# A two-block transformer kernel: 64 instead of 32 tokens of the expert layer go by gathered rows, and VectorE takes the low weight part first

## The chip, the core and the metric

The program runs on one core of a Trainium2 chip. The metric is the device time of one execution in microseconds: 3372.93 us before the change (median of 3 runs, 3371.32 to 3374.62). Engines are named as in the profile: PE is TensorE, PEld its weight loads, DVE is VectorE, ACT is ScalarE, POOL is GpSimd, SP is SyncE.

## What is computed

Two blocks over 256 tokens of width 2048 in f32. The change touches only the expert layer (PEER) of the first block. Each token has 8 heads, each head picks 16 of 16384 experts, and an expert is one row of `peer_u` and one of `peer_v`:

```python
expert = e1 * PEER_NKEYS + e2                 # 128 * 128 experts
gate = jax.nn.softmax(sv, axis=-1)            # over the 16 of a head
u = exp_u[ec]                                 # rows of 2048
a = jax.nn.gelu(jnp.einsum('cd,chkd->chk', xc, u))
w = gc * a
out = jnp.einsum('chk,chkd->cd', w, exp_v[ec])
```

After that come `x = x + g2 * out`, the final norm of the block and the whole second block (convolutions, gates, an MLP).

## The kernel before

**Two ways through the expert layer.** Most tokens go the dense way. The kernel multiplies them with all 16384 expert rows and masks the result with a routing matrix. The last `ROWS_T = 32` tokens go by rows. The kernel gathers the 128 rows that a token has picked, takes dot products with them, and adds the weighted rows of `peer_v`. `DENSE_T = 256 - ROWS_T = 224` is the number of columns of every dense matmul of the layer.

**The stream.** Weights come as units of 2 MB from HBM. A unit is split into two f16 halves. ACT writes the high part (`hi`, L1837, two instructions), and DVE the low part (`low`, L1077, two instructions). SP loads the next unit into a raw slot when the low part of the one before it there is done, and there are two raw and two split slots. PE then runs 96 matmuls of 128x128 weights per unit (L530, L531, L532). The layer has eight stages of 16 units: u0, u1, v0, u2, v1, u3, v2, v3. A u stage makes activations for one quarter of the experts, and a v stage sums one quarter into the output. One unit with what goes beside it is a *slot*. In slot n DVE makes the low part of unit n+2.

**Routing steps.** A stage that makes a quarter ready for its v stage (u1, v0, v1, v2) has `STEPS = DENSE_T // 16 = 14` routing steps, one per slot in slots 0 to 13. A step of 16 tokens is: DVE compares indices (`hot`: L1547 and L1549), POOL multiplies the first one-hot with the gates (`hot1_step`: L2209, twice), PE makes 32 small matmuls (`route`, L566), DVE multiplies with the activations (`gated`, L1556), ACT writes the high half (L2055), DVE the low half (`gated_low`, L1562). In a v stage DVE also adds the output to the residual (`residual_v`, L1568).

**Rows.** POOL's queue issues for each row token a gather (`row_load`, L2217, 128 rows of 8 KB, 1 MB) and, for the u rows, a load of the token's h vector copied to 128 partitions (`h_load`, L2222, 1 MB). DVE takes the dot product (`row_dot`, L1511) in u2, u3 and v3. PE multiplies with the v rows (`row_product`, L577) in v1, v2 and v3. POOL runs all of this and the 56 `hot1_step` calls in one written order. ACT does `row_gelu` and evicts the sum (`row_out`), PE turns it, and DVE adds it (`add_rows`, L1530 to L1539) near the end of v3. In u0 DVE also picks the experts (`select`, L1450 to L1486). The order on each engine is written out by hand, with semaphores between the engines.

The functions that the change touches:

Of the kernel before, what the change touches and what calls it, by code (L numbers as in the profile page):

```python
# [30 lines left out]
U32 = mybir.dt.uint32  # L31
# [23 lines left out]
ROWS_T = 32  # L55
# [129 lines left out]

def route_steps(n):

    return [n] if n < STEPS else []

ROW_GROUPS = [(0, 12), (12, 24), (24, 32)]
ROW_BATCHES = [(0, 12), (12, 24), (24, 28), (28, 32)]
ROW_LAST = {29: 0, 30: 1}

def row_loads():

    loads = []
    for n, (a, b) in enumerate(ROW_GROUPS):  # L200
        loads += [("u", i, i % 2) for i in range(a, b)]
        if n < 2:
            loads += [("v", i, i % 2) for i in range(a, b)]
        else:
            loads += [("v", i, ROW_LAST.get(i, 2)) for i in range(a, b)]
    place, count = {}, [0, 0, 0]
    for kind, i, buf in loads:
        count[buf] += 16
        place[kind, i] = (buf, count[buf])
    return place  # L210

ROW_PLACE = row_loads()

# [28 lines left out]
def program(nc, xT_d, wst, cst_d, dyn1_d, dyn2_d, dyn3_d, onehot_d, bmat_d, cmat_d, urow_d, vrow_d, skew_d, hrow_d, out_d):  # L244
    ctx = ExitStack()
    with ctx:
# [81 lines left out]
        row_buf = [A[:, 14336:16384], J[:, 0:2048], J[:, 4096:6144]]  # L328
        h_rep = J[:, 2048:4096]
        h_row = J[0:ROWS_T, 0:2048]  # L330
        ident16 = dyn[:, 320:384].bitcast(F16)
        dots = small[:, 0:ROWS_T]
        row_w = [h_rep[:, 0:384], h_rep[:, 0:384], J[:, 6144:6272], J[:, 6272:6400]]
        row_w = [w.rearrange("p (i t) -> p i t", t=ROWS_T) for w in row_w]
        row_out = J[:, 2048:2560]
        row_tmp = J[:, 2560:3072]
        x_rows = X[:, :].rearrange("p (k t) -> p k t", k=KT)[:, :, DENSE_T:T]
# [13 lines left out]
        row_index = gates.rearrange("p q h c -> p (q h c)").bitcast(U32)[:, 0:ROWS_T]  # L351
# [38 lines left out]
        def key_scores(h):  # L390
# [40 lines left out]
        row_in = [sem(f"row_in{i}") for i in range(3)]  # L431
# [4 lines left out]
            sem("rows_added"))  # L436
        merged, out_ready, relu_sb = sem("merged"), sem("out_ready"), sem("relu_sb")
# [49 lines left out]
        def _(pe_):  # L487
# [55 lines left out]
            def unit_u(s, bank):  # L543

                for m in range(2):
                    for k in range(KT):
                        hl = tuple(half[:, 0:DENSE_T] for half in halves(H, k))
                        mm = product(psW[:, bank, m * T:m * T + DENSE_T], s, k * 256 + m * P, hl, k == 0, k == KT - 1)
                return mm
# [417 lines left out]
            for u in range(32):  # L967
# [3 lines left out]
                if u == 0:  # L971
                    key_head(7)
                for qb in range(2):
                    if u == 9 + 8 * qb:
                        turn_picks(qb)
                if u >= 16:
                    for step_n in route_steps(u - 16):
                        route(step_n)
                if 20 <= u < 24:
                    h_rows(u - 20)  # L980
            for q in range(4):
                v0 = FIRST[f"v{q}"]
                pe_.wait_ge(acts_ready, STEPS * (q + 1))
                for n in range(16):
# [1438 lines left out]
```

## Time and profile before

| | us |
|---|---|
| median of 3 runs | 3372.93 |
| the profiled execution | 3384.46 |
| its span, first to last instruction | 3381.6 |
| PE busy | 3246.4 (96%) |
| DVE busy | 2354.0 (70%) |
| ACT busy | 1231.1 (36%) |
| POOL busy | 623.1 (18%) |

The expert layer starts with the first matmul of u0 at 718.92 us and ends with the first matmul of the next stage (z) at 2072.12 us. That is 1353.2 us of the span. PE's busy share is a poor guide here, since its instructions overlap and their ends are modelled. Starts of the same instruction one unit apart tell the pace. A row of the timeline gives start and duration in us, then engine, line, operation, output and input names with shapes, a count, and in brackets the idle time before it and what ended it. Because DVE instructions overlap a little at their ends, what one costs its successor is the distance of two starts.

A row of the windows view gives a stretch of the span and its length in us, the busy time of PE, PEld, DVE, ACT and POOL in it (with the number of instructions), the granted clock of PE as a share of 2.4 GHz, the busy share of the 16 DMA engines, and GB/s.

### The profile page before, as it was taken

The page shows a single profiled execution, that of the slowest core. Times are in us where ns is not written, and L with a number is a line of the kernel's source. Part 1 is how long each engine was busy: PE and PEld are TensorE (multiplying, and loading weights), DVE is VectorE, ACT ScalarE, POOL GpSimd, SP SyncE. Part 2 cuts the span into 40 slices and gives each one's busy share as a digit, 9 for nine tenths or more (in the row PEclk, how much of TensorE's full clock was granted, in tenths as well). Part 3 has the DMA queues.
Part 4 walks back from the last instruction along what each step waited for, and adds up shares of the span by engine and source line. Part 5 has one row for each costly group of instructions (what it writes and reads, how often), then busy time and mean ns, then how long its engine had stood idle before and what let it go on. Part 6 is the DMA issues. An engine that isn't in the chain of part 4 may idle for free.

```text
span 3381.6 us, 70432 instructions
## 1 busy us (share of the span) xinstructions
PE 3246.4 (96%) x31230; PEld 2906.9 (86%) x31230; DVE 2354.0 (70%) x2542; ACT 1231.1 (36%) x1126; POOL 623.1 (18%) x390
## 2 busy tenths in 40 slices
PE   7999999999999999999999988999999999999998
PEld 4777768789899999899989967888888788888887
DVE  7596145799998966895689667478758665554444
ACT  2010142444444444334433424344443433333332
POOL 0276000000354512471247110020000000000000
PEclk9899999999999999999999989999999999999999
DMA  9557694445455579777978884555545455555553
GB/s 410 236 222 293 278 419 153 175 175 217 183 201 202 203 290 423 278 278 297 426 261 289 349 321 175 199 199 199 198 175 202 172 199 198 201 199 205 202 203 132
DMA packets 66046, 814.77 MB, mean 241 GB/s; under 512 B 7354, under 2 KB 9418, under 8 KB 10512
## 3 DMA queue, kind: packets, MB, share of 16 engines
q1 hardware_dynamic: 48528, 700.47, 54.6%
q0 software_dynamic: 15008, 109.10, 8.3%
q8 instruction: 173, 2.83, 0.3%
q10 hardware_dynamic: 2304, 2.10, 0.2%
q14 instruction: 33, 0.27, 0.0%
HBM read 807.71 MB, written 3.93 MB: 240 GB/s over the span
## 4 chain that ended last, share of the span: by engine, by line
PE 73%; DVE 16%; DMA 7%; issue 2%; ACT 1%; ACTq 0%; DVEq 0%; POOL 0%; SPq 0%; POOLq 0%
PE psW L530 19%; PE psW L531 19%; PE psW L532 19%; PE psW L528 7%; DVE ring L1077 6%; DMA proj<-h_rows 6%; DVE proj L1549 2%; PE psW L628 1%; PE psM L628 1%; DMA ring<-wst_dram 1%; DVE arena L1511 1%; PE psM L577 1%; PE psM L782 1%; PE psM L566 1%; DVE proj L1511 1%
## 5 line engine op out<-in xcount | busy, mean ns | idle before, releaser
L1077 DVE SCALAR_TENSOR_TENSOR ring<-ring 128x2048 f16<-128x2048 f32 x526 | 1244.4, 2407 | 312.3 <-ACT ring L1837 310.7
L530 PE MATMUL psW<-h_act,ring 128*128 128x256 f16 (+1 forms) x5088 | 1366.5, 269 | 41.1 <-DVE ring L1077 19.7
L531 PE MATMUL psW<-h_act,ring 128*128 128x256 f16 (+1 forms) x5088 | 1366.3, 269 | 0.0
L532 PE MATMUL psW<-h_act,ring 128*128 128x256 f16 (+1 forms) x5088 | 1366.3, 269 | 0.0
L1837 ACT ACTIVATE ring<-ring 128x2048 f16<-128x2048 f32 x526 | 975.1, 1903 | 814.3 <-PE psW L532 727.9
L530 PE MATMUL psW<-arena,ring 128*128 128x224 f16 (+1 forms) x3072 | 816.3, 266 | 11.9 <-DVE ring L1077 10.9
L531 PE MATMUL psW<-arena,ring 128*128 128x224 f16 (+1 forms) x3072 | 815.8, 266 | 0.0
L532 PE MATMUL psW<-arena,ring 128*128 128x224 f16 (+1 forms) x3072 | 815.4, 265 | 0.0
L530 PEld LDWEIGHTS psW<-h_act,ring 128*128 128x128 f16 x5088 | 498.3, 98 | 98.4 <-issue 26.6
L532 PEld LDWEIGHTS psW<-h_act,ring 128*128 128x128 f16 x5088 | 499.5, 98 | 36.6
L531 PEld LDWEIGHTS psW<-h_act,ring 128*128 128x128 f16 x5088 | 498.8, 98 | 35.3
L530 PEld LDWEIGHTS psW<-arena,ring 128*128 128x128 f16 x3072 | 302.1, 98 | 54.2 <-issue 28.1
L532 PEld LDWEIGHTS psW<-arena,ring 128*128 128x128 f16 x3072 | 302.3, 98 | 13.2
L531 PEld LDWEIGHTS psW<-arena,ring 128*128 128x128 f16 x3072 | 302.1, 98 | 13.0
L2209 POOL TENSOR_TENSOR proj<-proj,cbias 128x512 f16<-128x512 f16 x56 | 157.3, 2828 | 492.7 <-DVE proj L1547 492.5
L528 PE MATMUL psW<-h_act,ring 128*128 128x256 f32 x896 | 202.8, 385 | 2.7 <-DVE h_act L1222 2.7
L528 PEld LDWEIGHTS psW<-h_act,ring 128*128 128x128 f32 x896 | 169.1, 192 | 32.0 <-issue 7.8
L2060 ACT ACTIVATE arena<-psW 128x448 f32<-128x448 f32 (+1 forms) x64 | 34.8, 543 | 339.5 <-PE psW L532 339.5
L2209 POOL TENSOR_TENSOR dyn<-proj,cbias 128x512 f16<-128x512 f16 x56 | 143.8, 2587 | 54.3 <-DVE proj L1547 54.1
L1549 DVE TENSOR_TENSOR proj<-dyn,work 128x2048 f16<-128x2048 f16 x56 | 132.0, 2358 | 0.0
L1780 DVE TENSOR_TENSOR work<-work 128x512 f32<-128x512 f32 x32 | 22.2, 693 | 125.5 <-ACT work L2148 125.5
L2148 ACT ACTIVATE work<-psW 128x512 f32<-128x512 f32 x32 | 19.1, 597 | 199.9 <-PE psW L532 199.9
(384 smaller groups left out, 2641.1 us busy)
## 6 DMA issues: line engine op xcount, KB each, us to landing
ring<-wst_dram SPq DMA_DIRECT2D x333, 2048.0 KB, 7.9
proj<-h_rows POOLq DMA_DIRECT2D x32, 1024.0 KB, 7.1
x_res<-xT_dram POOLq DMA_DIRECT2D x2, 2048.0 KB, 17.6
out_dram<-x_res SPq DMA_DIRECT2D x4, 512.0 KB, 2.9
bias_rows<-proj POOLq DMA_DIRECT2D x1, 1536.0 KB, 21.7
x_res<-cmat_dram POOLq DMA_DIRECT2D x1, 1024.0 KB, 5.3
x_res<-bmat_dram ACTq DMA_DIRECT2D x8, 128.0 KB, 3.7
h_act<-bias_rows ACTq DMA_DIRECT2D x8, 128.0 KB, 23.3
```

Of the source, the lines that this page charges most:

```text
L528: return nc.tensor.matmul(out, ring[:, w0:w0 + P], rhs, start=first, stop=last)
L530: nc.tensor.matmul(out, whi(s, col, P), xh, start=first, stop=False)
L531: nc.tensor.matmul(out, whi(s, col, P), xl, start=False, stop=False)
L532: return nc.tensor.matmul(out, wlo(s, col, P), xh, start=False, stop=last)
L566: mm = nc.tensor.matmul(psM[:, b, t * QUART_T:(t + 1) * QUART_T], hot2[b][:, t, :], hot1[b][:, t, r, :], start=(r == 0), stop=(r == 1))
L628: mm = nc.tensor.matmul(ada_bank(n)[32 * c:32 * c + 32, 0:256], csilu[:, k:k + 1].to_broadcast([P, 32]), ring[:, s * UNIT + k * 256:s * UN ...
L1077: ins = stt(wlo(s, c, n), ring[:, s * UNIT + c:s * UNIT + c + n], WSCALE, whi(s, c, n), ALU.mult, ALU.subtract)
L1511: v.tensor_tensor_reduce(row_buf[buf], row_buf[buf], h_rep, 1.0, 0.0, ALU.mult, ALU.add, dots[:, i:i + 1]).then_inc(dot_done, 1)
L1549: tt(hot2[b], iota16.unsqueeze(1).to_broadcast([P, STEP_T, P]), cols(1, P), ALU.is_equal).then_inc(hot2_ready, 1)
L1837: act(whi(s, p2 * (UNIT // 2), UNIT // 2), ring[:, c], ACT.Copy, scale=WSCALE).then_inc(hi_done, 1)
L2060: return act(A[:, span(a0, 2 * DENSE_T)].rearrange("p (m t) -> p m t", m=2), src, ACT.Gelu_apprx_tanh, scale=1 / WSCALE)
L2209: ins = g.tensor_tensor(hot1[n % 2][:, :, r, :], first1[n % 2], g16[:, r, STEP_T * n:STEP_T * (n + 1)].unsqueeze(2) .to_broadcast([P, STEP ...
```

## The change

- `ROWS_T` is 64, and the row tokens are the first 64, not the last 32. `DENSE_T` is 192, so the dense matmuls, the residual and the routed parts have 192 columns, and `STEPS` is 12. `ROUTE_AT` puts the steps in slots 0, 1, 2, 3, 5, 6, 7, 8, 10, 11, 12 and 14.
- A gather holds one head of a group of 8 tokens (8 x 16 = 128 rows) in place of all heads of one token. There are still 1 MB per gather and one gather per row token, so 64 for u and 64 for v. The h vectors of a group are loaded once (8 loads of 1 MB in place of 32).
- Row work is spread over seven stages by tables of slots (`DOT_AT`, `PRODUCT_AT`). Three buffers are filled in the order in which they are used (`ROW_LOADS`).
- Lists for the gathers are made in u0: `row_masks` and `take_list` on DVE, `row_lists` on PE, one copy on ACT.
- POOL's gate multiplications move to DVE, as the last two instructions of `hot`. `hot` for the first two steps of a quarter is done at the end of the quarter before.
- In a slot DVE does `low` first, and `gated`, `hot`, `gated_low` and the rows follow it.

```diff
-ROWS_T = 32
+ROWS_T = 64
+GROUP_T = 8
+BATCH_T = 32
...
+ROUTE_AT = [14 * k // (STEPS - 1) for k in range(STEPS)]
...
+DOT_AT = spread([("u1", 3, 15, 8), ("v0", 1, 15, 8), ("u2", 0, 15, 16), ("v1", 1, 15, 6), ("u3", 0, 15, 16),
+                 ("v2", 1, 15, 8), ("v3", 0, 1, 2)])
+PRODUCT_AT = spread([("v0", 2, 15, 8), ("u2", 2, 15, 6), ("v1", 1, 15, 14), ("u3", 1, 15, 6), ("v2", 0, 15, 16),
+                     ("v3", 0, 4, 6), ("v3", 5, 10, 8)])
+GELU_AT = [DOT_AT[8 * g + 7] + 1 for g in range(ROWS_T // GROUP_T)]
+EVICT_AT = [PRODUCT_AT[32 * b + 31] + 1 for b in range(ROWS_T // BATCH_T)]
+ADD_AT = [16 * 7 + 1, EVICT_AT[1] + 1]
+ROW_LOADS = [load[1:] for load in sorted([(at + 0.8, "u", i) for i, at in enumerate(DOT_AT)]
+                                         + [(at + 1.0, "v", i) for i, at in enumerate(PRODUCT_AT)])]
+ROW_BUFS = 3
...
             def hot(q, n):
+                if n >= STEPS:
+                    q, n = q + 1, n - STEPS
+                if q == 4:
+                    return
...
                 tt(hot2[b], iota16.unsqueeze(1).to_broadcast([P, STEP_T, P]), cols(1, P), ALU.is_equal).then_inc(hot2_ready, 1)
+                v.wait_ge(first1_ready, STEPS * q + n + 1)
+                for r in range(2):
+                    gate = g16[:, r, ROWS_T + STEP_T * n:ROWS_T + STEP_T * (n + 1)].unsqueeze(2).to_broadcast([P, STEP_T, QUART_T])
+                    ins = tt(hot1[b][:, :, r, :], first1[b], gate, ALU.mult)
+                ins.then_inc(hot1_ready, 1)
...
+            def take_list(b):
+                v.wait_ge(row_ps, b + 1)
+                tmp = row_part.rearrange("p (x k) -> p x k", k=TOPK)
+                step(tt(tmp, row_bank[b].rearrange("p (x k) -> p x k", k=TOPK), slot16.unsqueeze(1).to_broadcast([P, 32, TOPK]),
+                        ALU.mult))
+                step(v.tensor_reduce(rs[:, 32 * b:32 * b + 32], tmp, AX_X, ALU.add))
...
                 for n in range(16):
                     residual_v(q - 1, n)
                     steps = route_steps(n)
+                    low(v0 + n + 2)
                     for k in steps:
                         gated(q, k)
-                        if k + 2 < STEPS:
-                            hot(q, k + 2)
-                    low(v0 + n + 2)
-                    for k in steps:
+                        hot(q, k + 2)
                         gated_low(q, k)
+                    rows(f"v{q - 1}", n)
...
+            for n, (kind, i) in enumerate(ROW_LOADS):
+                if n >= ROW_BUFS:
+                    last, j = ROW_LOADS[n - ROW_BUFS]
+                    g.wait_ge(dot_done if last == "u" else row_used, j + 1)
+                    if last == "u" and j % HEADS == HEADS - 1 and j + 1 < ROWS_T:
+                        h_load(j // HEADS + 1)
+                row_load(kind, i)
```

DVE's order in one slot of v0 before (one slot is residual, `gated`, two of `hot`, `low`, `gated_low`):

```order
995 L1568 SCALAR_TENSOR_TENSOR x_res<-psW,mod,x_res 128x224
996 L1556 SCALAR_TENSOR_TENSOR work<-psM,arena 128x512
997 L1547 TENSOR_TENSOR proj<-dyn,work 128x512
998 L1549 TENSOR_TENSOR proj<-dyn,work 128x2048
999 L1077 SCALAR_TENSOR_TENSOR ring<-ring 128x2048 x2
1000 L1562 TENSOR_TENSOR arena<-work,arena 128x32x16
```

The same engine in a slot of v0 after, one with a routing step and a dot product (L1653 is the residual, L1125 `low`, L1641 `gated`, L1627 to L1633 `hot`, L1647 `gated_low`, L1577 the dot product):

```order
974 L1653 SCALAR_TENSOR_TENSOR x_res<-psW,mod,x_res 128x192
975 L1125 SCALAR_TENSOR_TENSOR ring<-ring 128x2048 x2
976 L1641 SCALAR_TENSOR_TENSOR work<-psM,arena 128x512
977 L1627 TENSOR_TENSOR proj<-dyn,work 128x512
978 L1629 TENSOR_TENSOR proj<-dyn,work 128x2048
979 L1633 TENSOR_TENSOR dyn<-proj,cbias 128x16x32 x2
980 L1647 TENSOR_TENSOR arena<-work,arena 128x32x16
981 L1577 ISA arena,rs<-arena,proj 128x2048
982 L1577 ISA rs 128x1
```

The low part has moved ahead of the routing work, two gate multiplications have come in, and a dot product has come into a stage that had none.

POOL's order around the end of u2's row work and the start of v1's before (L2217 a gather, L2222 the load of h, L2209 the gate multiplications):

```order
200 L2217 DMA arena<-urow_dram,gates 128x2048
201 L2222 DMA proj<-h_rows 128x2048
202 L2217 DMA proj<-urow_dram,gates 128x2048
203 L2222 DMA proj<-h_rows 128x2048
204 L2209 TENSOR_TENSOR proj<-proj,cbias 128x16x32 x2
205 L2217 DMA arena<-vrow_dram,gates 128x2048
206 L2209 TENSOR_TENSOR dyn<-proj,cbias 128x16x32 x2
```

POOL's order in u2 after (L2310 a gather, L2315 the load of h for the next group of 8):

```order
183 L2310 DMA arena<-urow_dram,rs 128x2048
184 L2310 DMA proj<-urow_dram,rs 128x2048
185 L2310 DMA arena<-urow_dram,rs 128x2048
186 L2310 DMA arena<-vrow_dram,rs 128x2048
187 L2310 DMA proj<-urow_dram,rs 128x2048
188 L2315 DMA proj<-h_rows 128x1x2048
189 L2310 DMA arena<-urow_dram,rs 128x2048
```

POOL's computing has gone from these stages, the loads of h are one in eight dot products, and gathers of u and v rows are mixed in one queue.

## Rows read from the trace of the kernel before

**Rows 1.** Windows: program start, u0, u1, v0, u2, inside u2, v1, v3.

```profile
30.00:60.00 30.00, 25.59 (x232) 14.09 (x236) 29.62 (x31) 7.49 (x15) 0.17 (x1) 0.89 1.01 427
...
718.90:879.30 160.40, 152.01 (x1549) 148.61 (x1548) 155.19 (x286) 74.03 (x57) 0.00 (x0) 0.99 0.56 207
879.30:1051.80 172.50, 164.59 (x2021) 162.56 (x2020) 158.88 (x100) 75.88 (x67) 83.90 (x29) 0.98 0.55 199
1051.80:1220.40 168.60, 161.90 (x1986) 159.94 (x1985) 155.33 (x103) 67.20 (x47) 88.28 (x31) 0.99 0.59 220
1220.40:1371.90 151.50, 148.47 (x1540) 146.75 (x1538) 98.99 (x57) 66.86 (x48) 24.54 (x21) 1.00 0.89 365
1303.20:1362.00 58.80, 56.25 (x579) 54.75 (x576) 40.24 (x24) 25.74 (x19) 12.78 (x11) 1.00 1.01 425
1371.90:1552.10 180.20, 175.02 (x2081) 162.91 (x2082) 158.19 (x106) 67.05 (x48) 108.52 (x43) 0.98 0.77 277
...
1883.30:2072.10 188.80, 162.79 (x1610) 151.11 (x1608) 129.52 (x148) 65.45 (x42) 17.02 (x21) 0.93 0.78 301
```

**Rows 2.** Timeline of PE: first matmuls of units in u2 (224 columns) and z (256).

```profile
1220.43 0.26 PE L530 MATMUL psW<-h_act,ring 128*128 128x224 f16 x1
...
1229.63 0.26 PE L530 MATMUL psW<-h_act,ring 128*128 128x224 f16 x1
...
2118.83 0.27 PE L530 MATMUL psW<-h_act,ring 128*128 128x256 f16 x1
...
2129.31 0.27 PE L530 MATMUL psW<-h_act,ring 128*128 128x256 f16 x1
```

**Rows 3.** Timeline of DVE, one slot of v0.

```profile
1098.70 0.68 DVE L1556 SCALAR_TENSOR_TENSOR work<-psM,arena 128x512 f32<-128x512 f32 x1
1099.29 0.68 DVE L1547 TENSOR_TENSOR proj<-dyn,work 128x512 f16<-128x512 f16 x1
1099.89 2.28 DVE L1549 TENSOR_TENSOR proj<-dyn,work 128x2048 f16<-128x2048 f16 x1
1102.09 6.18 DVE L1077 SCALAR_TENSOR_TENSOR ring<-ring 128x2048 f16<-128x2048 f32 x2
1108.19 0.68 DVE L1562 TENSOR_TENSOR arena<-work,arena 128x512 f16<-128x512 f32 x1
1108.80 0.44 DVE L1568 SCALAR_TENSOR_TENSOR x_res<-psW,mod,x_res 128x224 f32<-128x224 f32 x1
```

**Rows 4.** Timeline of POOL, the same slot of v0, then one of v1.

```profile
1100.05 6.07 POOL L2209 TENSOR_TENSOR dyn<-proj,cbias 128x512 f16<-128x512 f16 x2 [4.39 <-DVE proj L1547]
...
1423.13 3.08 POOL L2217 DMA_INDIRECT proj<-vrow_dram,gates  x1 [2.71 <-PE psM L577]
```

**Rows 5.** Timeline of PE between two units of v1: routing, row product.

```profile
1420.87 0.96 PE L566 MATMUL psM<-dyn,proj 128*128 128x32 f16 x32
1421.76 1.07 PE L577 MATMUL psM<-proj 128*32 128x512 f32 x8
```

**Rows 6.** Timeline of DVE in u2: a dot product, then the low part.

```profile
1296.01 2.29 DVE L1511 CUSTOM_DVE_ANT_0 arena<-arena,proj 128x2048 f32<-128x2048 f32 x1 [3.15 <-DMA proj<-h_rows]
...
1298.23 4.49 DVE L1077 SCALAR_TENSOR_TENSOR ring<-ring 128x2048 f16<-128x2048 f32 x2
```

**Rows 7.** DMA issues, 1303 to 1362 us (u2): KB each, median us to landing.

```profile
ring<-wst_dram SPq DMA_DIRECT2D x6, 2048.0 KB, 10.5
proj<-h_rows POOLq DMA_DIRECT2D x6, 1024.0 KB, 7.1
proj<-urow_dram,gates POOLq DMA_INDIRECT x3, 11.8
```

**Rows 8.** Timeline of PE in u0: a unit behind a wait, 3.4 us later.

```profile
820.82 0.27 PE L530 MATMUL psW<-h_act,ring 128*128 128x224 f16 x1 [2.28 <-DVE ring L1077]
...
824.19 0.40 PE L530 MATMUL psW<-h_act,ring 128*128 128x224 f16 x1
824.38 0.40 PE L531 MATMUL psW<-h_act,ring 128*128 128x224 f16 x1
```

More of the change, by code:

```diff
@@ L975, in _ @@
                         turn_picks(qb)
+                if u == 9:
+                    for b in range(3):
+                        row_lists(b)
+                if u == 11:
+                    row_lists(3)
                 if u >= 16:
@@ L1482, in select @@
                         yield
+                if qb == 0:
+                    step(stt(row_pick, pick[:, 0, :], float(P), pick[:, 1, :], ALU.mult, ALU.add))
                 v.wait_ge(gexp, qb + 1)
@@ new lines, in rows, with add_rows @@
+            def rows(name, n):
+                for g in slots(GELU_AT, name, n):
+                    row_weights(g)
+                for i in slots(DOT_AT, name, n):
+                    row_dot(i)
+            def add_rows(b):
+                v.wait_ge(row_T, b + 1)
+                t = slice(BATCH_T * b, BATCH_T * (b + 1))
+                tmp = row_tmp.rearrange("p (j c t) -> p j c t", j=4, c=4)
+                gain = mod[:, 80:96].rearrange("p (c j) -> p j c", c=4).unsqueeze(3).to_broadcast([P, 4, 4, BATCH_T])
+                step(tt(tmp, psM[:, b, :].rearrange("p (j c t) -> p j c t", j=4, c=4), gain, ALU.mult))
+                x = x_rows[:, :, t]
+                by_j = x.rearrange("p (c j) t -> p j c t", c=4)
+                step(tt(by_j, by_j, tmp, ALU.add))
@@ L1591, in _ @@
                     v.wait_ge(bank_free, FIRST["u1"] + 4)
+                low(FIRST["u0"] + u + 2)
                 for n in steps:
                     gated(0, n)
[L1594 to L1597 removed]
+                    hot(0, n + 2)
                     gated_low(0, n)
+                if u >= 16:
+                    rows("u1", u - 16)
             for q in range(1, 4):
                 v0 = FIRST[f"v{q - 1}"]
[L1602 to L1605 removed]
                 for n in range(16):
@@ L1639, in _ @@
                     low(FIRST["v3"] + j + 2)
-                if j < 8:
-                    row_dot(24 + j)
-                if j in (5, 9):
-                    row_weights(2 + (j == 9))
-                if j == 14:
-                    add_rows()
+                rows("v3", j)
+                for b in slots(ADD_AT, "v3", j):
+                    add_rows(b)
             inverse_rms(4)
```

310 lines of the change are left out of this document (148 added, 162 removed).

## The prediction

> **What bounds the kernel now.** I read the windows by stage first. The expert layer takes 1353.2 of the 3381.6 us of the span, from 718.9 to 2072.1, and its stages have different limits [rows 1]. In u0 DVE is busy 155.19 of 160.40 us. In v0 it is busy 155.33 of 168.60 us, and in u1 158.88 of 172.50 us. In u2 DVE has 98.99 of 151.50 us, and the DMA engines are the full ones. Over 58.8 us of u2 their share is 1.01 at 425 GB/s. In v1 PE is busy 175.02 of 180.20 us. v3 has 188.80 us and a clock of 0.93, the sign of long waits. There the chain of waits alternates between dot products and loads of h, as it does late in u2. u3 and v2 repeat u2 and v1 (151.0 and 180.2 us).
>
> Next come the paces. A unit of 224 columns takes 9.20 us and one of 256 takes 10.48 [rows 2]. Over 96 matmuls that is 95.8 and 109.2 ns, so 32 columns are 13.3 ns and the remainder is 2.5 ns. With 192 columns a matmul is 82.5 ns and a unit **7.92 us**, as long as the weight loads go on hiding. They do in the routing matmuls, where 32 of them with full 128x128 weights and 32 columns take 0.89 us by starts, 28 ns each [rows 5].
>
> In v0 one DVE slot is closed, each instruction starting as the one before ends. By starts, `gated` costs 0.59, `hot` 0.60 and 2.20, the low part 6.10, and `gated_low` 0.61 [rows 3]. With the residual it comes to 10.46 us a slot. The same low part costs 4.4 us in u2 (4.49 busy) [rows 6]. In v0 POOL's two gate multiplications run beside it from 1100.05 to 1106.12, so they span most of the low part [rows 4]. They therefore cost DVE 1.7 us a step, and the change removes them from POOL.
>
> **Part 1, the row lists in u0.** DVE is the bound, so all of it counts. A 128x512 instruction costs 0.6, a 128x128 one about 0.3. Four `take_list` of two 128x512 instructions with a wait for each result are 5.4 us. The masks are six small ones with two waits, 2.0 us; the packed index 0.3. `hot` for the first step moves in whole: 0.60 + 2.20 + two gate multiplications. These have not run on DVE. The nearest row is L1547, which has the same shape and type, at 0.60. The low bound is 0.3 (half of that), the high bound is POOL's own 3.0 each [rows 4]. I take 0.60, because L1547 is DVE's own with a broadcast operand as well. So a `hot` is 4.0 us. The sum is 5.4 + 2.0 + 0.3 + 4.0 = 11.7, and u0 goes from 160.4 to **172.1**. PE's shorter units, `h_rows`, and the lists' matmuls sit inside DVE's time.
>
> **Part 2, u1 and v0.** A routing step costs DVE 0.6 + 4.0 + 0.61 = 5.2 us, the low part 4.4, a dot product 2.22 [rows 6], and the residual 0.33. u1 has 16 low parts, 12 steps, 8 dots and 1.1 us of `weights16`: 70.6 + 62.5 + 17.8 + 1.1 = 152.0. v0 has 75.8 (with the residual) + 62.5 + 17.8 + 0.6 = 156.7. PE needs 16 x 7.92 = 126.7, plus 12 routes of 0.8 to 0.9 and 8 row products of 1.0 to 1.1 in v0 [rows 5]. That is 136 and 145, so DVE bounds both. The first slot of u1 stays long (about 16 us: the end of `select`, the second `hot`, the low part), and some 10 us of DVE's last slot fall after u2's first matmul. Together 16 + 152.0 + 156.7 - 10 = **314.7**, against 341.1 now. What is gained is POOL's interference (25 steps at 1.7 us), two steps less in each stage, and the `hot` pair at each stage's start. The 16 dot products and the gate multiplications eat most of it.
>
> Putting the low part first costs nothing here. In a DVE-bound slot its input is ready anyway, and PE gets it before the 5 us of routing work, so DVE may run a few us late without stopping PE.
>
> **Part 3, u2 and u3.** DVE needs 70.6 + 16 x 2.22 + 1.2 = 107 and PE 126.7 + 6 x 1.09 = 133.2 us. The transfers are 16 units of 2.10 MB, 22 gathers and two h loads of 1.05 MB, so 58.7 MB. At 425 GB/s [rows 1] that is **138** us. A raw slot also has a loop. From a low part's end its reload has two slots less 6.4 us (ACT's first half plus the low part) to land, and with the landing of 10.5 us [rows 7] that makes (10.5 + 6.4)/2 = 8.5 a slot, 136. With the gather's 11.8 it would be 9.1, 146. I take **142** for each, with ends 133 and 154. An h load now comes once in 8 dots, but the next dot is due one slot later. 7.1 us of landing stand against about 6 us of distance, so I allow 1 us for each of four such places.
>
> The Trainium skill ("DMA: Bandwidth & Descriptors", section "Where 436 GB/s comes from") speaks against this stage. It says that for HBM to SBUF about 358 GB/s per core binds. By that, u2 would be 164 us, slower than now. The rows of 425 and 427 GB/s contradict it.
>
> **Part 4, v1 and v2.** PE: 126.7 + 9.6 + 14 x 1.09 = 151.6 and with 16 products 153.7. DVE: 75.8 + 62.5 + 6 x 2.22 + 1.2 = 152.8. In v2, 8 dots, and two `hot` fewer since no quarter follows: 149. They are level, so I take the larger plus some: **155** and **157**, now 180.2 each. Of the 25 us a stage, 20.5 are PE's 32 columns. POOL's 3.08 us for the descriptors of a gather [rows 4], 1.5 times a slot, leave it half idle.
>
> **Part 5, v3.** Now a dot waits for its h load and PE for the last rows. After: 15 x 7.92 + 14 x 1.09 + 1.2 for two turns = 135.3, plus 2.3 where the second `add_rows` (about 5.6 us on DVE) exceeds the slack of its slot (seven instructions of 512 elements at 0.6 to 1.0). The last slot and the tail take 19.4 now (from PE's start of unit 15 at 2052.7 to z at 2072.1). They lose 1.3 of PE, and 3.1 because `add_rows` no longer stands before the last residual, which starts 3.1 us after its unit's end: 15.0. Sum **152.6**, now 188.8.
>
> **Sum.** 172.1 + 314.7 + 142 + 155 + 142 + 157 + 152.6 = 1235.4, so 117.8 less than 1353.2. I take off 9 us because DVE and PE work in v0, v1 and v2 don't match slot by slot, and the 4 us for the h loads. That leaves **105 us**. The profiled execution took 3384.46 (span 3381.6) and would take 3279. The runs' median lies 11.5 lower, and a difference should carry over. 3372.93 - 105 = **3268 us**.
>
> **Rivals.**
> *The raw slots and the gathers starve each other in u2 and u3.* The landing of the stream rises from 10.5 to 14 or so, because there are up to three gathers in flight where there were two with one h load. Then a slot is (14 + 6.4)/2 = 10.2 us, and u2 and u3 are 163 each, 42 more in all: 3310. For it: DMA is at 1.01 already. Against: the bytes per slot fall from 4.19 to 3.67 MB. 11%.
> *The clock.* Behind a gap of 2.28 us the granted clock fell to the lower level (1.2 GHz) for about 3 us: matmuls 0.19 apart, where they are 0.096 apart at 2.4 GHz [rows 8]. That is about 1.7 us a time. With shorter units PE waits in more DVE-bound slots (u0, u1, v0). Most of it is hidden, since DVE is the bound there. In v0 to v2 it is not, and 20 times 1.7 is 34: 3302. 8%.
> *Distinct bytes come slower.* Of u2's 4.19 MB a slot 1.05 were one row of h, read 128 times, so the distinct bytes came at 3.14 MB per 9.8 us (six h loads in 58.8 us [rows 1, 7]), 320 GB/s. If that was the ceiling, u2 and u3 take (58.7 - 2.1)/0.320 = 177 us each, v1 174, v2 187, and v3's first eleven slots 125 in place of 102: 142 more, 3410, slower than now. Against it stands the program's start, where the weight stream alone moves 427 GB/s [rows 1], all of it distinct. 3%. The skill's 358 GB/s, named above, is the mild form of it and would give 3334.
> *Better than forecast.* u2 and u3 at PE's 133 and no slot mismatch: 31 less, 3237. 8%.
> *Slower than before.* One mechanism: three buffers filled in order of use, so a gather is issued only when the third before it is consumed. If landing plus waiting to be used exceeds three uses, every dot holds up the low part behind it. 128 loads at 4.8 us each ((11.8 + 2.6)/3) is 614 us of the roughly 1000 available. It decides from about 25 us of landing, where each costs 9 us. At 28 us of landing: 128 x 10.2 = 1306 us from the first dot at about 940, so the layer ends near 2265, some 190 later than now: 3563. 11.8 is far from that. 2%. That the change doesn't do what it says (POOL still computing beside the low part) the order excludes.
>
> **Numbers.** The forecast with its own spread, 3250 to 3295, has 68%. For 8 in 10 the range goes from 3243 to 3312, which takes in both ends of the u2 term and the first two rivals. A measurement of this kernel can tell about 0.2% (7 us) from no change. Faster 0.95, within 0.01, slower 0.04.
>
> **What the profile after would show.** Units 7.92 us apart where PE is the bound. Low parts of 4.4 us by starts in u1, v0 and v1. Gate multiplications at 0.6 on DVE. v0 near 158 with DVE busy over 95%. u2 near 142 with a DMA share near 1. No wait of a dot for h rows over 3 us. v3 near 153 with a clock over 0.97. I would be wrong first in u2 and u3 (landing of the stream over 12 us), next in u0 (lists costing over 12 us), and in v1 and v2 if DVE and PE add up where I let them overlap.

## The result, and the profile after

The changed kernel takes **3463.53 us** (median of 4 runs, 3451.84 to 3465.41). The kernel before took 3373.77 beside it (4 runs). The ratio is 1.0253, with a 95% interval of 1.024 to 1.0267. It is 2.5% slower where I had forecast 3268 us, 3.1% faster. The profiled execution took 3465.41 us, with a span of 3463.6.

The busy times on the page:

```profile
PE 3150.6 (91%) x31266; PEld 2771.0 (80%) x31266; DVE 2365.0 (68%) x2695; ACT 1229.0 (35%) x1124; POOL 363.2 (10%) x318
```

The windows by stage, in the order of [rows 1]: u0, u1, v0, u2, 18 us inside u2, v1, v2, v3.

```profile
715.82:887.58 171.76, 145.52 (x1613) 140.94 (x1611) 166.09 (x306) 78.36 (x65) 0.58 (x1) 0.94 0.54 197
887.58:1056.75 169.17, 144.90 (x1924) 142.59 (x1924) 161.11 (x132) 74.74 (x63) 25.11 (x11) 0.95 0.75 272
1056.75:1228.33 171.58, 154.11 (x1985) 143.22 (x1985) 155.62 (x136) 65.15 (x45) 21.99 (x16) 0.94 0.81 293
1228.33:1411.34 183.01, 141.46 (x1588) 131.72 (x1585) 111.00 (x72) 67.44 (x52) 29.54 (x24) 0.88 0.89 322
1238.00:1256.00 18.00, 14.26 (x173) 14.03 (x171) 5.00 (x4) 7.22 (x7) 3.59 (x2) 0.99 1.01 272
...
1411.34:1596.61 185.27, 158.32 (x2037) 142.40 (x2033) 152.14 (x135) 65.91 (x46) 31.68 (x21) 0.92 0.82 303
1780.04:1987.24 207.20, 160.38 (x2053) 142.10 (x2049) 149.86 (x130) 65.47 (x45) 41.59 (x25) 0.89 0.78 294
1987.24:2152.57 165.33, 146.95 (x1664) 131.16 (x1661) 119.93 (x140) 64.40 (x41) 19.96 (x16) 0.96 0.79 310
```

The layer takes 1436.8 us in place of 1353.2. u0 is as forecast, and v3 did get shorter. u2 and u3 (183.4) are 32 us longer than before though PE has less to do in them. The window inside u2 shows a full DMA share of 1.01, as in [rows 1], at 272 GB/s instead of 425.

A DVE slot of v0, the answer to [rows 3]:

```profile
1097.15 0.68 DVE L1641 SCALAR_TENSOR_TENSOR work<-psM,arena 128x512 f32<-128x512 f32 x1
1097.76 0.68 DVE L1627 TENSOR_TENSOR proj<-dyn,work 128x512 f16<-128x512 f16 x1
1098.35 2.28 DVE L1629 TENSOR_TENSOR proj<-dyn,work 128x2048 f16<-128x2048 f16 x1
1100.56 1.29 DVE L1633 TENSOR_TENSOR proj<-proj,cbias 128x512 f16<-128x512 f16 x2
1101.76 0.69 DVE L1647 TENSOR_TENSOR arena<-work,arena 128x512 f16<-128x512 f32 x1
1102.36 0.41 DVE L1653 SCALAR_TENSOR_TENSOR x_res<-psW,mod,x_res 128x192 f32<-128x192 f32 x1
1102.69 4.49 DVE L1125 SCALAR_TENSOR_TENSOR ring<-ring 128x2048 f16<-128x2048 f32 x2
```

Everything in it costs what the forecast said. The two gate multiplications (L1633) take 1.29 us together (1.20 by starts), and the low part 4.49 where it took 6.18.

Where PE is the bound, the units do start 7.92 us apart. Then one starts 25.2 us after the one before it, 17.3 us late. PE's timeline in u2 (against [rows 2]):

```profile
1236.26 0.25 PE L553 MATMUL psW<-h_act,ring 128*128 128x192 f16 x1
...
1244.17 0.25 PE L553 MATMUL psW<-h_act,ring 128*128 128x192 f16 x1
...
1267.49 1.94 PE L602 MATMUL psM<-arena,h_act 128*32 128x512 f32 x8 [15.23 <-DMA arena<-vrow_dram,rs]
1269.36 0.34 PE L553 MATMUL psW<-h_act,ring 128*128 128x192 f16 x1
```

POOL and DVE at that place (POOL before: [rows 4], DVE before: [rows 6]):

```profile
1236.73 0.65 POOL L2315 DMA_DIRECT2D proj<-h_rows  x1 [16.28 <-DVE rs L1577]
1237.68 0.98 POOL L2310 DMA_INDIRECT arena<-urow_dram,rs  x1 [0.30 <-issue]
1238.97 2.92 POOL L2310 DMA_INDIRECT proj<-urow_dram,rs  x1 [0.30 <-issue]
1260.14 2.76 POOL L2310 DMA_INDIRECT arena<-vrow_dram,rs  x1 [18.25 <-DVE rs L1577]
```

```profile
1257.57 2.29 DVE L1577 CUSTOM_DVE_ANT_0 arena<-arena,proj 128x2048 f32<-128x2048 f32 x1 [13.76 <-DMA proj<-h_rows]
1259.79 0.08 DVE L1577 DVE_READ_ACCUMULATOR2_ANT rs<- 128x1 f32 x1
1259.79 4.49 DVE L1125 SCALAR_TENSOR_TENSOR ring<-ring 128x2048 f16<-128x2048 f32 x2
```

Read them together. The load of the next eight h rows is issued at 1236.73 and lands at 1257.44, 20.7 us later, where the forecast had 7.1 [rows 7]. Its sixteen landing events (updates of its semaphore) fall into two halves: eight come 5.2 to 6.3 us after the issue, and eight 15.8 to 20.7 us after it. DVE's dot waits 13.76 us for it. POOL's next item is a v gather into the buffer which that dot frees, so POOL waits too. PE then waits 15.23 us for this gather. The low part after the dot takes 4.49 us, as forecast.

The waits over the layer's stages (engine, line <- what was waited for: us in total, times, longest):

```profile
POOL arena L2310 <- DVE rs L1577: 439.1, 35, 30.8
POOL proj L2310 <- DVE rs L1577: 306.7, 21, 25.6
...
PE psM L602 <- DMA arena<-vrow_dram,rs: 111.6, 18, 20.9
...
PE psM L602 <- DMA proj<-vrow_dram,rs: 58.4, 9, 20.8
...
DVE arena L1577 <- DMA proj<-h_rows: 28.4, 2, 14.6
...
DVE proj L1577 <- DMA proj<-h_rows: 14.2, 2, 7.8
```

So PE waits 170.0 us for v rows and DVE 42.6 us for h. The forecast had 4 us for the h loads and nothing for the v rows. Two theories came from this. **A**: the grouped h load itself is slow. **B**: in POOL's one in-order queue, v gathers wait for buffers that a late dot frees, or stand behind another load that does.

### The profile page after: what moved, and what is told of

It reads as the page before. It is cut to its first block, busy times and chain, and to the rows that moved or that the text cites. A ratio compares the mean times of both kernels' runs of the same rounds, so it can differ in the third digit from the quotient of the medians.

```text
span 3463.6 us, 70500 instructions
## 1 busy us (share of the span) xinstructions
PE 3150.6 (91%) x31266; PEld 2771.0 (80%) x31266; DVE 2365.0 (68%) x2695; ACT 1229.0 (35%) x1124; POOL 363.2 (10%) x318
## 4 chain that ended last, share of the span: by engine, by line
PE 63%; DVE 19%; DMA 11%; issue 3%; ACT 2%; POOL 1%; ACTq 0%; DVEq 0%; SPq 0%; POOLq 0%
PE psW L553 16%; PE psW L555 16%; PE psW L554 16%; DVE ring L1125 8%; PE psW L551 7%; DMA arena<-vrow_dram,rs 5%; DMA ring<-wst_dram 3%; DMA proj<-vrow_dram,rs 2%; ACT ring L1922 2%; PE psW L673 1%; PE psM L602 1%; PE psM L673 1%; DVE proj L1629 1%; PE psM L827 1%; DVE arena L1577 1%
## 5 line engine op out<-in xcount | busy, mean ns | idle before, releaser
L1125 DVE SCALAR_TENSOR_TENSOR ring<-ring 128x2048 f16<-128x2048 f32 x526 | 1182.1, 2289 | 396.0 <-ACT ring L1922 393.8
L553 PE MATMUL psW<-h_act,ring 128*128 128x256 f16 (+1 forms) x5088 | 1351.1, 266 | 74.1 <-DVE ring L1125 50.6
L554 PE MATMUL psW<-h_act,ring 128*128 128x256 f16 (+1 forms) x5088 | 1351.2, 266 | 0.0
L555 PE MATMUL psW<-h_act,ring 128*128 128x256 f16 (+1 forms) x5088 | 1350.5, 265 | 0.0
L553 PE MATMUL psW<-arena,ring 128*128 128x192 f16 (+1 forms) x3072 | 790.4, 257 | 6.8 <-DVE arena L1647 3.7
L554 PE MATMUL psW<-arena,ring 128*128 128x192 f16 (+1 forms) x3072 | 789.9, 257 | 0.0
L555 PE MATMUL psW<-arena,ring 128*128 128x192 f16 (+1 forms) x3072 | 789.3, 257 | 0.0
L553 PEld LDWEIGHTS psW<-h_act,ring 128*128 128x128 f16 x5088 | 504.6, 99 | 144.6 <-DVE ring L1125 54.5
L555 PEld LDWEIGHTS psW<-h_act,ring 128*128 128x128 f16 x5088 | 505.7, 99 | 37.3
L554 PEld LDWEIGHTS psW<-h_act,ring 128*128 128x128 f16 x5088 | 504.6, 99 | 35.7
L602 PE MATMUL psM<-arena,h_act 128*32 128x512 f32 x368 | 59.0, 721 | 111.6 <-DMA arena<-vrow_dram,rs 111.6
L2145 ACT ACTIVATE arena<-psW 128x384 f32<-128x384 f32 x64 | 31.3, 489 | 332.2 <-PE psW L555 332.2
L1577 DVE CUSTOM_DVE_ANT_0 arena<-arena,proj 128x2048 f32<-128x2048 f32 x40 | 91.5, 2288 | 28.7 <-DMA proj<-h_rows 28.4
L1629 DVE TENSOR_TENSOR proj<-dyn,work 128x2048 f16<-128x2048 f16 x48 | 109.9, 2289 | 0.0
L602 PEld LDWEIGHTS psM<-arena,h_act 128*32 128x32 f32 x368 | 8.5, 115 | 119.3 <-issue 118.9
## 6 DMA issues: line engine op xcount, KB each, us to landing
ring<-wst_dram SPq DMA_DIRECT2D x333, 2048.0 KB, 11.4
```

Source lines behind the costliest of these rows:

```text
L553: nc.tensor.matmul(out, whi(s, col, P), xh, start=first, stop=False)
L554: nc.tensor.matmul(out, whi(s, col, P), xl, start=False, stop=False)
L555: return nc.tensor.matmul(out, wlo(s, col, P), xh, start=False, stop=last)
L602: mm = nc.tensor.matmul(psM[32 * c:32 * c + 32, 2, :], row_w[:, 8 * (g % 4) + h, :], row_buf[buf][:, 512 * c:512 * c + 512], start=(i % BA ...
L1125: ins = stt(wlo(s, c, n), ring[:, s * UNIT + c:s * UNIT + c + n], WSCALE, whi(s, c, n), ALU.mult, ALU.subtract)
L1577: v.tensor_tensor_reduce(row_buf[buf], row_buf[buf], h_rep, 1.0, 0.0, ALU.mult, ALU.add, dots[:, g, h:h + 1]).then_inc(dot_done, 1)
```

## Experiments

Where a time has no interval it is one run. Single runs of the kernel before lie between 3368.7 and 3384.7 us beside them, so the difference of two single times is uncertain by some 10 us. The profiles give a second measure: from the first matmul of u0 to the first of z, the expert layer alone. The rest of the span, which no edit touches, varies from 2019.9 to 2029.9 us.

| | layer, us |
|---|---|
| before | 1353.2 |
| e17, before with the low part first | 1332.5 |
| the changed kernel | 1436.8 |
| e1, no rows | 1145.5 |
| e2, one h row | 1362.9 |
| e8, h stored 16 times | 1371.8 |
| e9, h load on ScalarE's queue | 1439.7 |
| e4, order of loads alone | 1358.5 |
| e11, e8 with the order | 1299.6 |
| e13 and e19, e11 with the dot first | 1278.6, 1281.0 |
| e14, no dots | 1197.2 |
| e15, no products | 1243.0 |
| e16, stored twice | 1310.5 |
| e18, e16 with the low part behind | 1320.1 |
| e20, rows in turn | 1307.8 |
| e21, eight loads | 1324.4 |
| e24, distinct rows as 16 x 8 | 1313.7 |
| e25, h load as a gather | 1273.0 |

**Floor: no row work.** The edit takes out every row_dot, row_weights, row_product, gelu, eviction and row DMA, so the output lacks these tokens' expert part.

> Leaves out the 64 tokens' row work after the lists: no gathers, no loads of h copies, no dots, weights, products or additions of rows (so these tokens' output lacks its expert part); the 192-column part is unchanged. Both theories (A: the grouped h load; B: the in-order ring of three buffers on POOL) say that the dense part is as forecast and only rows make it late: about 3200 us, u1+v0 and u2, v1, u3, v2 with units of PE 7.9 us apart where nothing is routed, no unit above 12 us apart after u0. Rival C, the dense part itself is slower than forecast (VectorE's slot with hot1 on it, or units of PE that wait for weights): above 3300 us, and the long gaps stay.

Measured 3168.5 us. u2 and u3 take 126.7 and 126.8 us, 16 units of 7.92. u1 153.0, v0 142.6, v1 142.0, v2 141.0, v3 141.7. Rival C (a slow dense part) falls, and the rows cost 295 us of the 3463.5. The dense part is as forecast in u0, u2 and u3. u1 and v0 together take 295.6 us without a single dot, where the forecast less its two times 17.8 us of dots comes to 279.1. That sum was 16.5 us too low, and no run says which part of it.

**Theory A: three forms of the h load.**

```diff
 one row:     g.dma_start(h_rep, bass.AP(hrow_d.tensor, i * GROUP_T * D_MODEL, [[0, P], [1, D_MODEL]]))
 stored 16x: +g.dma_start(hrow_d, h_row.unsqueeze(1).to_broadcast([ROWS_T, TOPK, D_MODEL]))
             +g.dma_start(h_rep, bass.AP(hrow_d.tensor, i * P * D_MODEL, [[D_MODEL, P], [1, D_MODEL]]))
 on ACT:     +a.dma_start(h_rep, bass.AP(..., [[D_MODEL, GROUP_T], [0, TOPK], [1, D_MODEL]])).then_inc(h_rep_act, 16)
```

> The h load of a group reads one row (its first token's) and writes it to all 128 partitions, as the kernel before did, in place of 8 rows to 16 partitions each; it leaves out that the dots of the other 7 tokens use their own h. Same bytes written, same count of loads, same queue. Theory A: the pattern of 8 x 16 is what makes it land in 15 to 22 us; here it lands in about 7 us, the gathers behind it in about 12, VectorE's 42.6 us of waiting for it go, and the time falls by 60 to 110 us, to about 3375. Theory B: what is dear is the order on POOL's queue; the load's landing shortens but the time falls by less than 35 us, to above 3430.

> h rows are stored 16 times each in DRAM in u0 (8.4 MB in place of 0.5), so that the grouped load reads 128 rows that lie one behind the other; everything is computed. Theory A: as with one row, 7 us landing, about 3375 us plus at most 10 for the larger store. Theory B: above 3430. Rival D, distinct bytes instead of repeated ones are what makes the load slow: landing stays above 14 us and the time within 20 us of the changed kernel, while the one-row load is fast.

> The loads of groups 1 to 7 are issued by ScalarE (its own hardware queue) behind its wait for the group's eight dots, with the pattern 8 x 16 unchanged; everything is computed. Theory A (pattern): landing stays at 14 to 20 us, time within 20 us of the changed kernel's 3463. Rival E, POOL's software queue is what makes it slow: landing falls to 8 us or less and the time falls by over 50 us. Theory B allows a little: the gathers are issued one descriptor run (1 to 3 us) earlier, at most 10 us in all.

Measured 3392.4, 3394.2 and 3465.6 us. With 128 outermost the load lands in 5.4 to 10.4 us, whether its rows are one or 128, and 69 to 71 us go (74 and 65 by the layer, 7 us of e8's being the larger store: u0 178.9 instead of 171.8). On ScalarE's queue with the 8 x 16 pattern nothing is gained: it lands in 18.9 to 27.7 us, and a dot waits up to 21.46 us for it. It is the form of the load, not POOL's queue (rival E) and not distinct bytes (rival D).

**Theory B: the order on the queue, and where the dot stands.** In e8, with the h load mended, PE still waits 74.3 + 43.9 = 118.2 us for v rows. POOL, then PE, in v2:

```profile
1806.96 2.84 POOL L2310 DMA_INDIRECT proj<-urow_dram,rs  x1 [21.01 <-DVE rs L1577]
1810.10 1.89 POOL L2310 DMA_INDIRECT arena<-vrow_dram,rs  x1 [0.30 <-issue]
1812.30 0.94 POOL L2310 DMA_INDIRECT arena<-vrow_dram,rs  x1 [0.31 <-issue]
```

```profile
1822.47 1.94 PE L602 MATMUL psM<-arena,h_act 128*32 128x512 f32 x8 [9.55 <-DMA arena<-vrow_dram,rs]
```

The v gathers had their buffers, but stood behind a u gather that waited 21.01 us for a dot's buffer. The table sorts this dot's load by its slot, and DVE comes to the dot some 10 us later (4.4 us of low part and 5.2 of routing go before it).

```diff
-ROW_LOADS = [... sorted([(at + 0.8, "u", i) for i, at in enumerate(DOT_AT)]
+ROW_LOADS = [... sorted([(at + 1.9, "u", i) for i, at in enumerate(DOT_AT)]
```

and for "dot first":

```diff
                     low(v0 + n + 2)
+                    row_dots(f"v{q - 1}", n)
                     for k in steps:
                         gated(q, k)
```

> h rows stored 16 times (as in e8, 3394 us) and in the order of loads a dot's gather sorts by its slot + 1.9 in place of + 0.8: a dot runs about 10 us after its slot's unit, so that product n's gather no longer takes a buffer that the dot of slot n - 2 frees 7 us before it. Everything is computed. Theory B (POOL's in-order ring): PE's waits for v gathers (118 us in e8) fall below 60 and the time to about 3330 (3310 to 3350). Rival F (the queues' bandwidth: 24 MB of rows in a v stage, whatever the order): waits stay near 118 and the time within 20 us of 3394.

> As e11, and in the stages with routing the dot runs right behind the low part, ahead of the routing step's gated and hot parts (5 to 6 us earlier). Theory B: POOL's waits for dots shorten and another 10 to 25 us go, about 3310. Rival G, the dots now hold up VectorE's routing work, for which ScalarE and PE wait: 0 to 30 us slower than e11. Rival F: near 3394.

> The changed kernel with one edit, the order of loads (a dot's gather sorts by its slot + 1.9 in place of + 0.8); the h load stays 8 rows x 16 partitions. Everything is computed. If the two causes add, the time falls as from e8 to e11, by 72 us, to about 3392. If the slow h load delays the v gathers whatever their order (queued bytes), less of it comes, 30 to 50 us: 3415 to 3435. If the new order mends the gathers behind the h load too (they are issued earlier), more: under 3370.

Measured 3322.6, 3300.3 and 3381.6 us. The order alone takes 71.6 us from e8, and 82 from the changed kernel (72.2 and 78.3 by the layer). Within the noise of single runs the two causes add. Putting the dot first takes another 22 by single runs, 13 by e13's timed median below, 19 to 21 by the layer. The same waits in e11:

```profile
PE psM L602 <- DMA arena<-vrow_dram,rs: 24.0, 6, 8.4
...
PE psM L602 <- DMA proj<-vrow_dram,rs: 8.7, 4, 5.0
```

118.2 us have become 32.7, and in e13 they are 18.5. Rivals F (bandwidth) and G (the dots hold up the routing work) fall.

**One side of the rows alone.** e14 has only the `v` entries in ROW_LOADS and leaves out the dots and h loads. e15 has only the `u` entries, on the base of e8, and leaves out the products. Both outputs lack a part.

> Leaves out the dots with their gathers of u rows, the loads of h copies and the gelu of the dots (weights are made of the gates alone); v gathers, products and additions stay, in the same slots. Theory B: nothing on POOL's queue waits for a dot, PE's waits for v gathers fall below 10 us, and the time is 3168.5 (no rows) plus 64 products of about 1.1 us = 70 at most: 3215 to 3245. Rival F: 64 gathers alone do not fill the queues either, so it would be fast here too, but e15 with the other 64 would be slow by itself. Rival H, PE waits for something else of the v side (weights, eviction): above 3270.

> Base e8 (h stored 16 times). Leaves out the gathers of v rows, the products, their eviction, transposes and additions; dots, weights, loads of h stay, in the same slots. Theory B: 3168.5 plus 7 for the larger store plus the dots of the stages with routing, 30 x 2.22 = 67 where VectorE's slot is the longer one, nothing in u2 and u3: 3200 to 3245. With e14 this makes some 3290 for both kinds without their meeting on one queue, 100 below e8's 3394. Rival F: no more than that, but the meeting is then one of bandwidth. Rival: a late u gather stops VectorE for over 30 us in sum here too: above 3260.

Measured 3220.8 and 3267.6 us. e14 is as B has it: 64 gathers and products for 52 us, and no wait of PE for a v row. e15 missed its range by 23 us. No u row is waited for (h loads: 9.7 us), and yet u2 takes 139.3 us instead of 126.7, with ACT waiting 106.2 us for weights from DRAM over all stages. Both sides together add 52.3 + 99.1 (7 of it the larger store) = 151.4 to the floor: 3319.9, and e11 with both takes 3322.6. That these agree to 3 us is luck with single runs; by the layer it is 1294.7 and 1299.6. So with the right order little or nothing is left of their meeting on the queue. In e8 it cost 74 us (77 by the layer).

**Why the pattern is slow.** First came a split in 16 (rows stored twice), rows in turn, and eight loads.

```diff
 e16: +bass.AP(..., [[D_MODEL, 2 * GROUP_T], [0, TOPK // 2], [1, D_MODEL]])
 e20: +bass.AP(..., [[0, TOPK], [D_MODEL, GROUP_T], [1, D_MODEL]])
 e21: +for t in range(GROUP_T): g.dma_start(h_rep[TOPK*t:TOPK*(t+1), :], bass.AP(..., [[0, TOPK], [1, D_MODEL]]))
```

> As e13 (3300 us), with each h row stored twice (1 MB) in place of 16 times, and read as 16 rows x 8 partitions in place of 8 x 16: the candidate for the fastest. Theory A1: the load is slow because its outermost dimension of 8 spreads it over 8 of the 16 DMA engines; with 16 it lands in 7 to 12 us as in e13, u0 comes back from 179 to 172 us, and the time is 3290 to 3298. Rival A2, reading one row 16 times by neighbouring packets is what is slow (8 times would be half as slow): landing above 10 us where e13 had 8, time 3310 to 3330.

> As e13 with the h rows stored once, and the h load reads 8 rows in turn, 16 times over (partition p gets row p mod 8), in place of each row 16 times in a run; it leaves out that a partition's dots use its own token's h. Theory A2a, a queue that reads one row again and again by itself is what makes packets slow (e16: 560 to 680 ns at 8 repeats, 309 in e13): here each queue goes over distinct rows, packets take 309 ns and the load lands in 8 to 13 us, time about 3293. Theory A2b, rows that several packets read at once are slow in whatever order, unless all read the same one: packets over 500 ns, time above 3315.

> As e13 with the h rows stored once, and a group's h load made of eight DMAs, one row to 16 partitions each, over all 16 queues; everything is computed. Theory A2a: no queue reads a row more than once in a run, packets take about 309 ns, landing 8 to 13 us plus what POOL takes to write eight descriptor lists (0.6 us each by the one of e13, 5 us), u0 at 172 us: about 3295, as fast as e13. Theory A2b, or lists that cost POOL over 2 us each: 3310 to 3340.

Measured 3329.1 us (ratio 0.9857, 0.9835 to 0.9878), 3334.2, and 3343.1 (0.9898, 0.9883 to 0.9913). I had expected e16 near 3294: A1 (eight idle queues) is not enough. e16's sixteen landing events come evenly (10.2 to 13.0 us after the issue at 1217.0), and the load is still slow (7.7 to 23.3 us over its eight). A2a falls with e20 and e21. e16 and e20 have 16 outermost, and e21 has eight DMAs of 16 partitions. The last pair crosses split and source:

```diff
 e24: +bass.AP(hrow_d.tensor, i * 2 * GROUP_T * HALF, [[HALF, 16], [D_MODEL, 8], [1, D_MODEL]])  # HALF = 8 rows + 64
 e25: +step(ts(h_index, h_index, 4, None, ALU.logical_shift_right))     # iota 128 g + p -> 8 g + p / 16
      +g.indirect_dma_start(h_rep, None, hrow_d[:, :], bass.IndirectOffsetOnAxis(ap=h_index[:, i:i + 1], axis=0))
```

> As e13 (3300 us; timed 3309), with the same 128 distinct rows in DRAM, but 64 elements of padding after each 8, so that the h load's pattern is 16 x 8 rows instead of 128; everything is computed. Theory P (destination): with 16 outermost each queue writes 8 partitions that follow each other, and two queues at a time get in each other's way: packets of 600 ns as in e16 and e20, half the rate, time 3325 to 3340. Theory S (source): only rows read several times are slow: 309 ns, landing 8 to 13 us, time within 12 us of e13's. The store of 8.4 MB stays, so u0 is 179 us in both.

> As e13 with the h rows stored once, and a group's h load made a gather: an index tile holds 8 g + p / 16 for partition p, so that each of 8 rows is read 16 times by the same 128-row form as the u and v gathers; everything is computed. Theory P: packets take 309 ns, the load lands in 8 to 13 us, u0 is 172 in place of 179, and the time is 3293 to 3303, the fastest so far; POOL's list costs 1 to 3 us in place of 0.57, up to 1 us a group. Theory S: packets of 500 to 900 ns as in the changed kernel or e16, 3325 to 3360.

Measured 3344.3 us and **3301.0** us (5 runs, 3296.5 to 3303.2; ratio 0.9772, 0.9758 to 0.9787). Theory S falls on both sides: distinct rows in the slow split are slow, and repeated rows in the fast one are fast. The split is the cause. That the slow splits collide at the destination, as theory P has it, fits but is not shown by these two. The load lands in 7.9 to 17.0 us in e25, three of eight times later than the 13 us I had expected, and u0 is back at 171.9. Windows of 8 us with the h load at the start of v0 under way, in the changed kernel, e16, e20, e24, and then e8 and e25 (the last column is GB/s):

```profile
1064.60:1072.60 8.00, 8.00 (x122) 8.00 (x121) 4.49 (x3) 3.71 (x2) 0.96 (x1) 1.00 1.04 289
```
```profile
1056.60:1064.60 8.00, 8.00 (x122) 8.00 (x121) 4.56 (x3) 3.71 (x2) 0.90 (x1) 1.00 1.00 303
```
```profile
1059.50:1067.50 8.00, 8.00 (x122) 8.00 (x120) 3.26 (x3) 3.71 (x2) 0.85 (x1) 1.00 1.01 302
```
```profile
1069.40:1077.40 8.00, 8.00 (x122) 8.00 (x120) 3.30 (x3) 3.71 (x2) 0.83 (x1) 1.00 1.02 304
```
```profile
1063.70:1071.70 8.00, 8.00 (x123) 8.00 (x121) 4.56 (x3) 3.71 (x2) 0.83 (x1) 1.00 0.98 414
```
```profile
1055.90:1063.90 8.00, 8.00 (x122) 8.00 (x120) 4.55 (x3) 3.71 (x2) 0.94 (x1) 1.00 0.99 418
```

The same in packets of 8 KB: POOL's DMA queue in 8 us of u2, of the changed kernel (1242 to 1250), e24 (1233 to 1241) and e25 (1217 to 1225). The columns are packets, MB, and their time as a share of 16 engines.

```profile
q0 software_dynamic: 199, 1.52, 100.1%
```
```profile
q0 software_dynamic: 136, 1.06, 58.4%
```
```profile
q0 software_dynamic: 184, 1.38, 41.7%
```

1.52 MB are 186 packets of 8 KB in 1.001 x 128 us, **0.69 us** each. In e24 it is 0.58, in e25 0.32 (the tiny rest are semaphore writes). These are means over the h load and the gathers beside it. In the changed kernel's stretch the weight stream moves nearly nothing (5 packets): its next unit is issued at 1243.45, and its first 16 KB packet starts at 1250.17. So POOL's slow packets have the DMA to themselves. The window:

```profile
1242.00:1250.00 8.00, 8.00 (x100) 8.00 (x98) 1.77 (x3) 4.09 (x3) 0.00 (x0) 1.00 1.01 193
```

**The slot's order.** e17 is the kernel before with `low` moved ahead of `gated` and `hot`. e18 is e16 with the reverse edit.

> The kernel before with one part of the change alone: VectorE's slot begins with the low part; rows, 32 at the end, one-hot gates on POOL, as before. Forecast's step: low parts no longer wait behind 5 us of routing, the stages v1 and v2 (180.2 us each) get shorter: 10 to 40 us faster than 3373. Rival, the stages with routing are bound by VectorE's sum (gated, one-hot, low, residual, slowed by POOL beside it): within 5 us of before, and the gain of the final version comes from the narrower dense part alone.

> As e16, with VectorE's slot as in the kernel before: the gated part and the one-hot operations of a routing step run ahead of the low part and the dot. Forecast's step: the low part first spares PE its wait in each of the 48 slots with a routing step that is PE-bound; here stages u1, v0, v1, v2 get 5 to 10 us longer each, 20 to 40 us in all. Rival: these stages are bound by VectorE's total of 9.8 to 13 us in a slot, whatever its order: within 8 us of e16.

Measured 3362.1 us (5 runs; ratio 0.9952, 0.9935 to 0.9969) and 3343.1. By these times the low part first is worth 14 to 16 us in either kernel, by the layer 20.7 in e17 and 9.6 in e18. In e17 it is mostly in v0 (162.4 instead of 168.6) and in v1 and v2 (175.5 and 175.8, from 180.2). e18 is one run and e16's four lie between 3323.1 and 3335.7, so there the size is rough. For e18 I had asked for 20 to 40.

**e13 timed.**

> The kernel of e13 once more (h rows stored 16 times, order of loads by slot + 1.9, dot behind the low part), now timed against the kernel before: 3300 us as in its one run, ratio 0.976 to 0.982. If single runs mislead: above 3320.

Measured 3309.3 us (5 runs, 3302.8 to 3311.8; ratio 0.9793, 0.9779 to 0.9808), 9 us above its single run, though its layer is only 2.4 us longer. e25 has the lowest median and the shortest layer of the complete versions here, 8 us each below this one. The intervals of the two ratios overlap slightly. The u2 and v1 of e25:

```profile
1216.00:1364.50 148.50, 136.65 (x1609) 129.07 (x1608) 108.69 (x69) 66.46 (x51) 39.96 (x26) 0.98 0.98 396
1362.00:1519.00 157.00, 152.31 (x2038) 139.28 (x2036) 149.87 (x134) 66.27 (x45) 40.08 (x21) 1.00 0.93 362
```

## Why the prediction was wrong, step by step

The stages sum to 1436.8 us where the prediction had 1235.4, 201 us off.

- **Part 1, u0 at 172.1: right** (171.8). The two gate multiplications are 1.20 us by starts, 0.6 each, as taken from L1547.
- **The paces: right.** Units 7.92 us apart, low parts 4.49 us in v0 beside nothing on POOL (against 6.18 in [rows 3]), dots 2.29.
- **Part 3, the h load: the first failed step.** "7.1 us of landing stand against about 6 us of distance, so I allow 1 us for each of four such places." The 7.1 belongs to a load with 128 outermost [rows 7]. The load of the change has 8 outermost, and I gave it the old one's price because its bytes and queue were the same. Over its eight it lands in 14.6 to 22.1 us. The waits it causes and the gathers behind it cost 69 to 71 us (e2, e8), not 4.
- **Parts 2 to 5, the v gathers: the second failed step, a wait that was not costed.** I took PE's row products as 1.09 us of work and asked only whether POOL had time for the descriptors ("1.5 times a slot, leave it half idle"). POOL is not busy but blocked: 745.8 us of waiting for dots. The table asks for dot n's row at slot n + 0.8, while the dot runs after the low, gated and hot parts, about one slot later, and three buffers leave no room for that. The order costs 72 us (e8 to e11) and the dot's place 13 to 22 us (e11 to e13).
- **The slower rival had the mechanism.** It named three buffers in order of use, but let it decide "from about 25 us of landing", with 2%. That point was worked out as if every load waited for the same three uses. At the gathers' ordinary landing (medians of 9.1 to 10.8 us in e8) the order already cost 72 us. In the rows of e8 above, the v gather goes out at 1810.10, only 2.8 us before PE is ready for the product. The time was between the forecast and this rival's 3563.
- **Distinct bytes (3%): refuted.** e8 reads 128 distinct rows at 414 GB/s, 98% of DMA share. The clock rival was a follower only: 0.88 in u2 behind the long gaps, and 0.98 there again in e25.
- **Raw slots and gathers that starve each other (11%): true in small.** In e25 a unit of weights lands in 11.4 us (median of u2 and of u3), where the forecast had 10.5 and this rival 14. The two stages stay under its 163 us.
- **Part 3, u2 and u3 at 142: too low by 5 to 10 us.** In e25 they take 148.5 and 152.4. The DMA share is 0.98, the rate 396 GB/s instead of the 425 of one good stretch [rows 1]. 58.7 MB at 396 are 148 us. This term was mis-sized and the mechanism right. Beside it, e25 has 323.6 us for u1 + v0 (forecast 314.7), 156.8 for v1 (155), 159.8 for v2 (157) and 159.9 for v3 (152.6).

With both failed steps mended, the kernel is where the forecast had it but for 33 us: 3301.0 against 3268. The stages of e25 sum to 1273.0, where the forecast had 1235.4 and 13 us on top for the mismatch and the h loads. So 24.6 us lie in the terms of the last point, u2, u3, and u1 + v0 above all, which were not tried one by one. The other 8 us lie outside the stages: the kernel before took 3376.7 beside e25, 4 more than the 3372.93 of the forecast, and the rest is not traced.

## What to carry to other kernels

Price a DMA by a row of the same access pattern, outermost dimension included, not by one of the same bytes. A load that must copy few rows to many partitions can be written as a gather with an index per partition (e25). In a shared in-order queue, sort each load by when its buffer's user really runs on its engine, and look at what is queued behind a load that waits: an engine that is 10% busy, as POOL is here, can still be the bound through its queue.

## What the runs showed that I had not expected

- A 1 MB DMA to 128 partitions lands in 6 to 10 us by a 128-row pattern (e8) and in 15 to 22 by an 8 x 16 one, on POOL's queue and no sooner on ScalarE's (e9). Meanwhile the weight stream can stand still: 193 GB/s in all at a share of 1.01. So a DMA share near 1 does not say that the bytes flow.
- Eight DMAs of 16 partitions (e21) have the same fault (305 GB/s) and cost POOL 0.5 us each.
- In the 128-row form the median 8 KB packet takes 309 ns whether its row is read once (e8), 16 times (e25) or 128 times (e2).
